# One Trainium2 core, a two-block transformer forward: the first gates' evacuation, the convolutions and their silus at other places of the hand-written order

## The chip, the cores and the metric

The kernel runs on one core of one Trainium2 chip. TensorE (PE) multiplies into PSUM banks; VectorE (DVE), ScalarE (ACT) and GpSimd (POOL) work beside it, SyncE (SP) issues DMAs. Each engine takes its own instructions in program order and waits on semaphores that other engines raise. The metric is device time in microseconds, lower is better. Before the change: 1570.03 us, median of three runs (1566.84 to 1570.04).

## The reference

One token block of 512 x 1024 goes through two layers. The first: a hybrid mixer, a cross-attention to 256 memory tokens, a squared-relu MLP. The second: a gated convolution beside a sliding-window attention, and a convolutional gated MLP. The change is in the mixer, whose core is

```python
proj = h @ w_in                       # gu, gv, q, k, v, gate, b_logit, a_logit
y_a = chunk_spatial_gating(gu, gv, ...)
qkv = silu(causal_dwconv(concat(q, k, v), dn_conv))      # 4 taps
q, k = l2norm(q), l2norm(k)                              # per head of 128
o = gated_delta_rule(q, k, v, g, beta)                   # 4 heads, triangular solves
o = rmsnorm(o, dn_onorm) * silu(gate)
out = concat(y_a, o) @ w_out
```

## The kernel before, in words

Activations lie transposed, 128 channels by 512 tokens in a tile. A projection of one output tile is 8 steps over the inner dimension, each three matmuls of 128x512 (L1308 to L1310), since weights and activations are split into a high and a low part (fp32r): 24 matmuls for a projection, 12 for a half. Projection j writes PSUM bank j mod 4 (banks 0 to 3) and may start only when the result of projection j-4 has left that bank (`evacuated`). Banks 4 to 7 are side banks; the small steps take them in turn (`side_turns`), and a step waits until the holder before it has been read.

Weights pass four slots. SP loads a slot when it is free; a `split` copies the high part on ACT (L1604) and then subtracts on DVE (L1884). SP's next load waits for both.

One list, `SCHEDULE`, sets the order of everything: `schedule()` writes (kind, number) steps, and each engine's program walks the list and issues its own share of every step. So where a step stands in the list sets its place in the queues of PE, ACT, DVE and POOL at once.

The steps that matter here (numbers 0 to 3 are heads; qkv tile n is q for 0 to 3, k for 4 to 7, v for 8 to 11):

- `conv n`: DVE takes the projection out of its bank (L1869), ACT scales it (L1667), DVE adds three taps (L1876).
- `shape n`: ACT applies silu (L1671), behind the taps. `sums n` (q and k): PE turns the tile (L1381), which needs `shape n`; ACT squares it with a sum (L1679).
- `gate n`: DVE takes the gate out of its bank (L1869 into `gate`), ACT applies silu (L1707). Gates 0 and 1 are projections 3 and 4, so gate 0 holds bank 3, the bank of projection 7 (k of head 1 is 6, v of head 1 is 7).
- The delta heads: `decay h` (PE L1235, ACT exp L1713, DVE L2030 and L2034, ACT exp L1716), `strict h` (PE L1411, nine DVE instructions, L2042 to L2059), `turn h` (PE L1420, DVE L2062), then `level_y` and `level_x` for levels 1 to 6 (PE L1437 and L1465/L1470; ACT copies y, L1721; DVE subtracts, L2089/L2090), `solve h`. The level_x of a level needs ACT's copy of y; the level_y of the next needs DVE's subtraction.
- `root` and `row` of the second block's first norm: PE turns the sum of squares that POOL has added up (L1229), DVE and POOL form the root, PE spreads it (L1235). They stand between the projections k2 and q2.

A projection is issued in halves, and the generators for projections and heads are advanced in turn, one half projection to one head step. On ACT, functions of different table sets (silu, exp, gelu) need an ACT_TABLE_LOAD between them.

Of the kernel before, what the change touches and what calls it, by code (L numbers as in the profile page):

```python
# [17 lines left out]
KT = D // P  # L18
# [4 lines left out]
H = 4  # L23
# [4 lines left out]
F2T = 2816 // P  # L28
# [10 lines left out]
SLOTS = 4  # L39
LEAD = SLOTS - 1  # L40
# [18 lines left out]

ON_DVE = (A_INPUT, *HALF_OF)  # L60

LAST_TILES = [slice(0, 3), slice(3, 6), slice(6, KT)]

GATES_BEHIND = {0: (0, 1), 1: (2,)}
# [64 lines left out]
N_LOADS = N_PROJ - KEPT  # L131
FIRST_EXTRA = N_LOADS - (KEPT - SLOTS)
PROJ = {(name, n, k0): j for j, (name, n, k0, k1) in enumerate(WEIGHTS)}
# [58 lines left out]
def schedule():  # L192

    out, done, split = [], set(), [0]

    def add(kind, n=0):
        out.append((kind, n))

    def split_ahead(j):
        while split[0] < min(j + LEAD + 1, N_LOADS) and (split[0] < SLOTS or split[0] - SLOTS in done or (  # L200
                split[0] >= FIRST_EXTRA and PROJ["gate2", F2T - 1, 0] in done)):
            add("split", split[0])
            split[0] += 1

    def project(name, n, k0=0, ka=None, kb=None):
        j = PROJ[name, n, k0]
        ka, kb = WEIGHTS[j][2] if ka is None else ka, WEIGHTS[j][3] if kb is None else kb
        if j < FRONT:
            done.add(j)
            return  # L210
        split_ahead(j)
        add("mm", (j, ka, kb))
        if kb == WEIGHTS[j][3]:
            done.add(j)
# [2 lines left out]
        add("split", j)  # L217
        split[0] = j + 1

    aside, convolved, normed_heads = [], [], []  # L220

    def halves_and_aside(name, n):
        project(name, n, kb=KT // 2)
        while convolved:
            add("shape", convolved.pop(0))
        if aside:
            aside.pop(0)()
        yield
        project(name, n, ka=KT // 2)
        if aside:  # L230
            aside.pop(0)()

    def conv_qkv(n):
        if PROJ["qkv", n, 0] not in done:
            yield from halves_and_aside("qkv", n)
        yield
        add("conv", n)
        convolved.append(n)

    def scaled(h):  # L240
        add("norms", h)
        normed_heads.append(h)

    def projections():
        for h in range(1, H):
            yield from conv_qkv(h)
            yield from conv_qkv(H + h)
            aside.extend([lambda h=h: add("sums", h), lambda h=h: add("sums", H + h), lambda h=h: scaled(h)])
            yield from conv_qkv(2 * H + h)
            for n in GATES_BEHIND.get(h, ()):  # L250
                yield from halves_and_aside("gate", n)
                add("gate", n)
                yield
        norm = memory_norm()
        for n in range(H):
            for name in GATING[n]:
                yield from halves_and_aside(name, n)
                if name == "gu":
                    if n == 0:
                        add("mix_bias")  # L260
                    add("spatial_u", n)
                else:
                    add("spatial_v", n)
                    aside.extend([lambda n=n: add("statistics", n), lambda n=n: add("normalise", n), lambda n=n: add("mix", n)])
                yield
                if n or name == "gv":
                    next(norm, None)
        last = halves_and_aside("gate", H - 1)
        next(last)
        for t in range(KT):  # L270
            add("stage", (A_MEMORY, t))
        yield
        for _ in last:
            pass
        add("gate", H - 1)
        yield
        while aside:
            aside.pop(0)()
            yield
# [57 lines left out]
    def first_memory_keys():  # L337
        yield from memory_keys(range(EARLY_KEYS))
# [35 lines left out]
    project("gate", 1, ka=KT // 2)  # L374

    ahead = PROJ["qkv", 1, 0]
    add("mm", (ahead, 0, 1))
    add("sums", H)
    add("decays")
    add("mm", (ahead, 1, KT - 2))  # L380
    first = delta_head(0)
    next(first)
    add("mm", (ahead, KT - 2, KT))
    done.add(ahead)
    add("sums", 0)
    scaled(0)
    add("shape", 2 * H)
    filler = itertools.chain(projections(), first_memory_keys())
    aside.extend([lambda: add("gate", 0), lambda: add("gate", 1)])
    in_flight, waiting = [first], list(range(1, H))  # L390
    while waiting or in_flight:
        next(filler, None)
# [37 lines left out]
    for n in range(2, KT):  # L430
        project("xa_wq", n)
        add("query", n)
        h = n // XT - 1
# [26 lines left out]
    for p, (k0, k1) in enumerate(FFN_PARTS):  # L460
# [7 lines left out]
        for n in range(KT):  # L468
            project("ffn_w2", n, k0)
            add("residual", (("ffn_w2", k0), n))  # L470
            if k1 == FT:
                normed(A_SECOND, n)
                add("square2", n)
    project("k2", 0)
    add("root", A_SECOND)
    project("q2", 0, kb=KT // 2)
    add("root", A_TWICE)
    project("q2", 0, ka=KT // 2)
    add("row", A_SECOND)

    for n in (QT, 0):
# [101 lines left out]
    add("row", A_LAST)  # L583
    for n in range(len(LAST_TILES)):
        add("final", (A_LAST, n))
# [225 lines left out]
def build_program(nc, x_in, mem_in, front_in, logits_in, weights_in, ws_in, columns_in, rows_in, sinks_in, matrices_in,  # L811
                  positions_in, out):
    with ExitStack() as base:
# [6 lines left out]
        def signal(name, kind, per=1):  # L820
            return Signal(semaphore(name), kind, per if callable(per) else lambda n: per)
# [45 lines left out]
        gate = sbuf("gate", [P, H, S], stack=delta)  # L867
# [28 lines left out]
        q2 = sbuf("q2", [P, QT, S], stack=second)  # L896
        k2 = sbuf("k2", [P, S], stack=second)
# [104 lines left out]
            signal("statistics_pe", "statistics"), signal("statistics_dve", "statistics", 2 * NC + 1), signal("statistics_pool", "statistics"))  # L1002
        normalise_dve = signal("normalise_dve", "normalise")
        mix_pe, mix_dve = signal("mix_pe", "mix"), signal("mix_dve", "mix", 2)
        gate_dve, gate_act = signal("gate_dve", "gate"), signal("gate_act", "gate")
        decay_pe, decay_act, decay_dve = signal("decay_pe", "decay"), signal("decay_act", "decay", 2), signal("decay_dve", "decay", 2)
        strict_pe, strict_dve = signal("strict_pe", "strict"), signal("strict_dve", "strict", 9)
        turn_pe, turn_dve = signal("turn_pe", "turn"), signal("turn_dve", "turn")
# [578 lines left out]
        def scalar_program(act):  # L1587
# [7 lines left out]
            for kind, n in SCHEDULE:  # L1595
                if kind == "split":
# [3 lines left out]
                    elif n >= SLOTS:  # L1600
                        name, i, k0, k1 = WEIGHTS[n - SLOTS]
# [100 lines left out]
                elif kind == "spatial_v":  # L1702
                    q.wait_ge(*spatial_v_dve.at(n))
                    act.activation(temp("v", n), temp("v", n), ACT.Gelu_apprx_tanh).then_inc(spatial_v_act.handle, 1)
                elif kind == "gate":
                    q.wait_ge(*gate_dve.at(n))
                    act.activation(gate[:, n, :], gate[:, n, :], ACT.Silu).then_inc(gate_act.handle, 1)  # L1707
                elif kind == "decay":
# [8 lines left out]
                elif kind == "level_y":  # L1717
                    h, level = n
# [126 lines left out]

            for n in range(0, len(LAST_TILES), 2):
                q.wait_ge(*final_dve.at((A_LAST, n)))
                act.dma_start(out_tiles[:, LAST_TILES[n], HALF_OF[A_LAST]], xs[:, LAST_TILES[n], HALF_OF[A_LAST]]).then_inc(out_landed.handle, 16)

        def vector_program(dve):  # L1850
# [28 lines left out]
            for kind, n in SCHEDULE:  # L1879
# [434 lines left out]
                elif kind == "final" and n[0] == A_LAST:  # L2314
                    tiles = LAST_TILES[n[1]]
                    part = xs[:, tiles, HALF_OF[A_LAST]]
# [71 lines left out]
        def sync_program(sp):  # L2388
# [131 lines left out]
```

## Time and profile before

| what | value |
|---|---|
| runs | 1566.84, 1570.03, 1570.04 us |
| the profiled execution: its time, its span | 1569.95 us, 1568.2 us |
| PE busy | 1543.0 us, 98% of the span |
| DVE, ACT, POOL busy | 878.0, 601.8, 104.9 us |
| granted TensorE clock, mean | 0.993 of full |
| HBM | 143.29 MB read, 93 GB/s over the span |

A busy PE share of 98% leaves only some 25 us of idle time to be had or lost, so the table of who waited for whom on PE, and the stretches of lower clock, say where a change of order can act. Most of them lie in the first 210 us.

### The profile page before, as it was taken

The numbers are of one execution on the slowest core, as the hardware profiler recorded it, in microseconds if no ns is written. First come the engines' busy times: TensorE is split into PE (matmuls) and PEld (weight loads), VectorE is DVE, ScalarE is ACT, GpSimd is POOL, SyncE is SP. The second block draws the span as 40 slices with busy tenths as digits, with TensorE's granted clock in tenths as the row PEclk, the third lists the DMA queues.
The fourth block names the chain that finished last, engine by engine and source line by source line (L and its number), as shares of the span: only waits on it lengthen the run. The fifth ranks groups of instructions, "written<-read, shape, count | busy, mean of one in ns | idle before, by whom it ended". The sixth has DMA issues, their size and how long they took to land.

```text
span 1568.2 us, 20461 instructions
## 1 busy us (share of the span) xinstructions
PE 1543.0 (98%) x8150; PEld 1275.4 (81%) x8150; DVE 878.0 (56%) x1331; ACT 601.8 (38%) x975; POOL 104.9 (7%) x91
## 2 busy tenths in 40 slices
PE   9898999999999999999999999999999999999998
PEld 7687789888788888888888877877888888888887
DVE  7676666654364344445565777644555663564465
ACT  6534333533344132322446344432334331332233
POOL 0000111220030000000040010100002000000000
PEclk9998999999999999999999999999999999999999
DMA  7211113531132322232332223221332233222221
GB/s 265 68 55 41 55 55 109 188 107 59 36 113 90 107 90 99 94 104 78 108 108 81 81 81 108 74 94 62 107 113 89 95 107 102 87 99 102 95 71 64
DMA packets 44941, 146.70 MB, mean 94 GB/s; under 512 B 5040, under 2 KB 8368, under 8 KB 44720
## 3 DMA queue, kind: packets, MB, share of 16 engines
q1 hardware_dynamic: 42448, 141.80, 26.8%
q10 hardware_dynamic: 2400, 3.61, 0.7%
q8 instruction: 65, 1.06, 0.3%
q14 instruction: 28, 0.23, 0.1%
HBM read 143.29 MB, written 2.10 MB: 93 GB/s over the span
## 4 chain that ended last, share of the span: by engine, by line
PE 87%; DVE 6%; ACT 4%; issue 3%; DMA 1%; POOL 0%; SPq 0%; DVEq 0%; POOLq 0%; ACTq 0%
PE bank L1308 26%; PE bank L1310 26%; PE bank L1309 26%; DVE w_lo L1884 1%; PE bank L1526 1%; PE bank L1543 1%; ACT w_hi L1604 1%; DVE temp L1876 1%; PE bank L1437 1%; PE bank L1465 1%; DVE temp L1869 1%; PE bank L1470 1%; PE bank L1273 0%; PE bank L1275 0%; PE bank L1274 0%
## 5 line engine op out<-in xcount | busy, mean ns | idle before, releaser
L1308 PE MATMUL bank<-a_hi,w_hi 128*128 128x512 f32 (+1 forms) x1275 | 499.3, 392 | 6.0 <-DVE gate L1869 6.0
L1310 PE MATMUL bank<-a_hi,w_lo 128*128 128x512 f32 (+1 forms) x1275 | 491.3, 385 | 0.0
L1309 PE MATMUL bank<-a_lo,w_hi 128*128 128x512 f32 (+1 forms) x1275 | 491.2, 385 | 0.0
L1884 DVE TENSOR_TENSOR w_lo<-w_raw,w_hi 128x1024 fp32r<-128x1024 f32 (+2 forms) x259 | 330.3, 1276 | 171.4 <-ACT w_hi L1604 171.0
L1604 ACT ACTIVATE w_hi<-w_raw 128x1024 fp32r<-128x1024 f32 (+2 forms) x259 | 267.0, 1034 | 198.3 <-PE bank L1310 195.0
L1308 PEld LDWEIGHTS bank<-a_hi,w_hi 128*128 128x128 f32 x1275 | 240.6, 189 | 57.5 <-issue 9.9
L1310 PEld LDWEIGHTS bank<-a_hi,w_lo 128*128 128x128 f32 x1275 | 240.4, 189 | 48.5
L1309 PEld LDWEIGHTS bank<-a_lo,w_hi 128*128 128x128 f32 x1275 | 240.9, 189 | 45.6
L1308 PE MATMUL bank<-b_hi,w_hi 128*128 128x512 f32 (+1 forms) x720 | 276.7, 384 | 0.4 <-ACT b_hi L1744 0.4
L1309 PE MATMUL bank<-b_lo,w_hi 128*128 128x512 f32 (+1 forms) x720 | 275.1, 382 | 0.0
L1310 PE MATMUL bank<-b_hi,w_lo 128*128 128x512 f32 (+1 forms) x720 | 275.1, 382 | 0.0
L1308 PEld LDWEIGHTS bank<-b_hi,w_hi 128*128 128x128 f32 x720 | 135.3, 188 | 28.4 <-issue 1.7
L1310 PEld LDWEIGHTS bank<-b_hi,w_lo 128*128 128x128 f32 x720 | 135.3, 188 | 26.3
L1309 PEld LDWEIGHTS bank<-b_lo,w_hi 128*128 128x128 f32 x720 | 135.4, 188 | 26.1 <-issue 0.2
L2156 DVE TENSOR_TENSOR xs<-xs,bank 128x512 f32<-128x512 f32 (+1 forms) x88 | 55.9, 637 | 135.0 <-PE bank L1310 130.9
L1869 DVE TENSOR_TENSOR temp<-bank,rstd 128x512 f32<-128x512 f32 x101 | 69.4, 687 | 62.5 <-PE bank L1310 58.0
L1876 DVE SCALAR_TENSOR_TENSOR temp<-temp,columns 128x512 f32<-128x512 f32 x96 | 72.3, 753 | 35.0 <-ACT temp L1841 17.2
L2344 POOL TENSOR_TENSOR square_sum<-square_sum,square 128x512 f32<-128x512 f32 x28 | 39.5, 1410 | 612.5 <-ACT square L1639 612.5
L2134 DVE TENSOR_TENSOR b_lo<-temp,b_hi 128x512 fp32r<-128x512 f32 x62 | 42.9, 692 | 59.3 <-ACT b_hi L1744 59.0
L1744 ACT ACTIVATE b_hi<-temp 128x512 fp32r<-128x512 f32 x62 | 39.2, 633 | 82.5 <-DVE temp L2313 56.7
L1784 ACT ACTIVATE temp<-temp 128x512 f32<-128x512 f32 x32 | 20.2, 632 | 89.4 <-DVE temp L2209 89.4
L2335 POOL TENSOR_TENSOR narrow<-narrow,columns 128x4 f32<-128x4 f32 (+1 forms) x13 | 18.5, 1423 | 422.0 <-DVE narrow L1927 382.9
(317 smaller groups left out, 1196.2 us busy)
## 6 DMA issues: line engine op xcount, KB each, us to landing
w_raw<-weights_in SPq DMA_DIRECT2D x247, 512.0 KB, 3.2
w_raw<-weights_in SPq DMA_DIRECT2D x8, 384.0 KB, 2.9
x_first<-x_in SPq DMA_DIRECT2D x8, 256.0 KB, 5.8
xs<-x_in ACTq DMA_DIRECT2D x8, 256.0 KB, 5.0
w_raw<-weights_in SPq DMA_DIRECT2D x8, 256.0 KB, 2.7
mem_x<-mem_in SPq DMA_DIRECT2D x1, 1024.0 KB, 7.7
out<-xs SPq DMA_DIRECT2D x8, 128.0 KB, 1.8
w_raw<-front_in SPq DMA_DIRECT2D x5, 192.0 KB, 6.1
```

The costliest lines, as they stand in the source:

```text
L1308: pe.matmul(to, weights_hi[:, at], hi, start=k == k0, stop=False)
L1309: pe.matmul(to, weights_hi[:, at], lo, start=False, stop=False)
L1310: t = pe.matmul(to, weights_lo[:, at], hi, start=False, stop=k == k1 - 1)
L1604: act.activation(split_weights(n)[0][:, 0:size], raw[:, n % SLOTS, 0:size], ACT.Copy).then_inc(split_act.handle, 1)
L1744: act.activation(b_hi[:, b_slot(g, i), :], x, ACT.Copy).then_inc(b_act.handle, 1)
L1784: act.activation(temp("relu", n), temp("relu", n), ACT.Square).then_inc(relu_act.handle, 1)
L1869: return dve.tensor_tensor(to, full(name, n, k0)[0:to.shape[0], 0:width], scale[0:to.shape[0], 0:width], ALU.mult)
L1876: dve.scalar_tensor_tensor(acc, buf[:, at:at + S], weight(i), acc, ALU.mult, ALU.add).then_inc(done.handle, 1)
L1884: dve.tensor_tensor(lo[:, 0:size], raw[:, n % SLOTS, 0:size], hi[:, 0:size].bitcast(F32), ALU.subtract).then_inc(split_dve.handle, 1)
L2134: dve.tensor_tensor(lo, x, hi.bitcast(F32), ALU.subtract).then_inc(b_dve.handle, 1)
L2156: dve.tensor_tensor(xs[:, t, tokens], xs[:, t, tokens], full(name, t, k0)[:, 0:tokens.stop - tokens.start], ALU.add).then_inc(residual_dve ...
L2344: pool.tensor_tensor(total, total, square("square", n)[:, 0:total.shape[1]], ALU.add).then_inc(square_pool.handle, 1)
```

## The change

It reorders steps; the work of each stays the same.

1. Gates 0 and 1 leave their banks right behind `decays`, ahead of `decay 0`; their silus (a step `silu` of its own now) stand behind `shape 8`. `norms 0` and `strict 0` come ahead of `sums 0`, and the first part of projection 5 is two inner steps long, not one.
2. The DVE work `conv n` comes half a projection later: between the halves of the next projection, behind the head's step. `shape n` comes another half later, ahead of the next `split`.
3. One call of `project` splits at most one weight tile.
4. `sums` of k, `statistics`/`mix` of group 0 are moved by a half.
5. The root of the second block's norm stands in the middle of k2, not behind it; the second root behind k2.
6. The last output tiles leave in four pieces (1, 2, 3 and 2 tiles), not three (3, 3, 2).

```diff
-LAST_TILES = [slice(0, 3), slice(3, 6), slice(6, KT)]
+LAST_TILES = [slice(0, 1), slice(1, 3), slice(3, 6), slice(6, KT)]
...
-    def split_ahead(j):
-        while split[0] < min(j + LEAD + 1, N_LOADS) and (split[0] < SLOTS or split[0] - SLOTS in done or (
-                split[0] >= FIRST_EXTRA and PROJ["gate2", F2T - 1, 0] in done)):
-            add("split", split[0])
-            split[0] += 1
+    def split_ahead(j, most=SLOTS):
+        for _ in range(most):
+            if split[0] < min(j + LEAD + 1, N_LOADS) and (split[0] < SLOTS or split[0] - SLOTS in done or (
+                    split[0] >= FIRST_EXTRA and PROJ["gate2", F2T - 1, 0] in done)):
+                add("split", split[0])
+                split[0] += 1
...
     def halves_and_aside(name, n):
-        project(name, n, kb=KT // 2)
         while convolved:
             add("shape", convolved.pop(0))
+        project(name, n, kb=KT // 2, most=1)
         if aside:
             aside.pop(0)()
         yield
-        project(name, n, ka=KT // 2)
+        while projected:
+            add("conv", projected[0])
+            convolved.append(projected.pop(0))
+        project(name, n, ka=KT // 2, most=1)
...
     def conv_qkv(n):
         if PROJ["qkv", n, 0] not in done:
             yield from halves_and_aside("qkv", n)
+        projected.append(n)
         yield
-        add("conv", n)
-        convolved.append(n)
...
-            aside.extend([lambda h=h: add("sums", h), lambda h=h: add("sums", H + h), lambda h=h: scaled(h)])
+            aside.append(lambda h=h: add("sums", h))
+            aside.extend([lambda: None, lambda h=h: add("sums", H + h), lambda h=h: scaled(h)])
...
-    add("mm", (ahead, 0, 1))
+    add("mm", (ahead, 0, 2))
     add("sums", H)
     add("decays")
-    add("mm", (ahead, 1, KT - 2))
+    for n in GATES_BEHIND[0]:
+        add("gate", n)
+    add("mm", (ahead, 2, 5))
     first = delta_head(0)
     next(first)
-    add("mm", (ahead, KT - 2, KT))
+    add("mm", (ahead, 5, KT))
     done.add(ahead)
+    scaled(0)
+    next(first)
     add("sums", 0)
-    scaled(0)
     add("shape", 2 * H)
+    for n in GATES_BEHIND[0]:
+        add("silu", n)
     filler = itertools.chain(projections(), first_memory_keys())
-    aside.extend([lambda: add("gate", 0), lambda: add("gate", 1)])
...
-    project("k2", 0)
+    project("k2", 0, kb=KT // 2)
     add("root", A_SECOND)
-    project("q2", 0, kb=KT // 2)
+    project("k2", 0, ka=KT // 2)
     add("root", A_TWICE)
-    project("q2", 0, ka=KT // 2)
+    project("q2", 0)
     add("row", A_SECOND)
```

What this makes of the queues, at three places. First DVE, about 42 to 60 us. `small` and `narrow` are per-head scalars, L1869 into `temp` is a projection taken out of its bank, into `gate` a gate. Before:

```order
L1957 TENSOR_TENSOR small<-small 128x16
L2030 TENSOR_TENSOR decays_t0<-bank6,small 128x512
...
L2059 TENSOR_TENSOR qkv<-qkv,temp2 128x512
L1869 TENSOR_TENSOR temp3<-bank1,rstd 128x512
L1967 MEMSET temp3 128x3
L1876 SCALAR_TENSOR_TENSOR temp4<-temp3,columns,temp4 128x512 x3
L1884 TENSOR_TENSOR w_lo<-w_raw,w_hi 128x1024 x2
L1869 TENSOR_TENSOR gate<-bank3,rstd 128x512
L1869 TENSOR_TENSOR gate<-bank0,rstd 128x512
```

And the same place now:

```order
L1970 TENSOR_TENSOR small<-small 128x16
L1882 TENSOR_TENSOR gate<-bank3,rstd 128x512
L1882 TENSOR_TENSOR gate<-bank0,rstd 128x512
L2043 TENSOR_TENSOR decays_t0<-bank6,small 128x512
...
L2072 TENSOR_TENSOR qkv<-qkv,temp2 128x512
L1987 TENSOR_SCALAR narrow<-narrow 128x4
L1897 TENSOR_TENSOR w_lo<-w_raw,w_hi 128x1024
L2075 COPY inv_b0<-bank6 128x256
L1882 TENSOR_TENSOR temp3<-bank1,rstd 128x512
```

The two gates stand ahead of the decay now; one split and the turn's copy stand ahead of the first convolution.

Second ACT, around the decay of head 2. L1721 (now L1734) copies a level's y, the L1713 pair (L1726) and L1716 (L1729) are the two exps of the decay, L1671 (L1684) a silu, L1604 (L1617) a split, L1679 (L1692) the squares of `sums`. Before:

```order
L1604 ACTIVATE w_hi<-w_raw 128x1024
L1671 ACTIVATE qkv<-temp4 128x512
L1679 ACTIVATE square1,narrow<-bank4 128x128 x4
L1721 ACTIVATE level_y1<-bank5 128x256
L1713 ACT_TABLE_LOAD
L1713 ACTIVATE temp0<-bank6 128x512
L1716 ACTIVATE decays_t0<-decays_t0 128x512
L1679 ACTIVATE square0,narrow<-bank7 128x128 x4
```

And now:

```order
L1734 ACTIVATE level_y1<-bank5 128x256
L1726 ACT_TABLE_LOAD
L1726 ACTIVATE temp3<-bank6 128x512
L1729 ACTIVATE decays_t0<-decays_t0 128x512
L1684 ACT_TABLE_LOAD
L1684 ACTIVATE qkv<-temp2 128x512
L1617 ACTIVATE w_hi<-w_raw 128x1024
L1692 ACTIVATE square1,narrow<-bank7 128x128 x4
```

The silu of tile 3 (q of head 3), the split and the squares of that tile stand behind both exps now, with a table load ahead of the silu.

Third PE at the second block's norm. Bank 0 is k2, bank 1 is q2, `square_sum` is what POOL adds up. Before:

```order
L1308 MATMUL bank0<-a_hi,w_hi 128x512
L1309 MATMUL bank0<-a_lo,w_hi 128x512
L1310 MATMUL bank0<-a_hi,w_lo 128x512
L1229 MATMUL bank4<-matrices,square_sum 128x128 x4
L1308 MATMUL bank1<-a_hi,w_hi 128x512
```

And now:

```order
L1321 MATMUL bank0<-a_hi,w_hi 128x512
L1322 MATMUL bank0<-a_lo,w_hi 128x512
L1323 MATMUL bank0<-a_hi,w_lo 128x512
L1242 MATMUL bank7<-matrices,square_sum 128x128 x4
L1321 MATMUL bank0<-a_hi,w_hi 128x512
```

The turn of the sum of squares is 12 matmuls earlier: bank 0 stands on both sides of it.

## Rows read from the trace of the kernel before

**Rows 1.** Waits of PE over the span: us in total, times, longest.
```profile
PE bank L1308 <- DVE gate L1869: 6.0, 1, 6.0
PE bank L1411 <- ACT square L1679: 2.8, 1, 2.8
PE bank L1420 <- DVE k_dec L2082: 1.7, 1, 1.7
PE bank L1470 <- DVE temp L2010: 1.4, 1, 1.4
...
PE bank L1381 <- ACT qkv L1671: 0.6, 1, 0.6
...
PE bank L1459 <- ACT level_y L1721: 0.5, 1, 0.5
PE bank L1229 <- DVE inv_t L2095: 0.5, 1, 0.5
...
PE bank L1411 <- DVE decays_t L2030: 0.4, 1, 0.4
```
**Rows 2.** Stretches: length, busy PE, PEld, DVE, ACT, POOL, granted clock, DMA share, GB/s.
```profile
55.70:62.60 6.90, 2.92 (x7) 2.37 (x8) 6.03 (x10) 3.80 (x6) 0.00 (x0) 0.51 0.46 151
...
137.60:141.10 3.50, 3.50 (x17) 3.50 (x17) 1.73 (x5) 0.00 (x0) 0.99 (x1) 0.51 0.00 0
...
151.30:158.10 6.80, 6.17 (x28) 4.99 (x29) 4.42 (x10) 1.57 (x2) 0.00 (x0) 0.50 0.22 79
```
**Rows 3.** Timeline of DVE, 48 to 60 us: start, length, instruction, idle before.
```profile
48.50 0.68 DVE L2042 TENSOR_TENSOR decays_t<-decays_t,small 128x512 f32<-128x512 f32 x1
...
52.86 0.68 DVE L1869 TENSOR_TENSOR temp<-bank,rstd 128x512 f32<-128x512 f32 x1
...
56.58 2.35 DVE L1884 TENSOR_TENSOR w_lo<-w_raw,w_hi 128x1024 fp32r<-128x1024 f32 x2
58.84 1.28 DVE L1869 TENSOR_TENSOR gate<-bank,rstd 128x512 f32<-128x512 f32 x2
```
**Rows 4.** Timeline of PE, 67.5 to 74 us.
```profile
68.38 0.68 PE L1465 MATMUL bank<-inv_tb,level_y 64*64 64x64 f32 x16
...
69.46 0.50 PE L1308 MATMUL bank<-a_hi,w_hi 128*128 128x512 f32 x1
...
72.43 0.68 PE L1437 MATMUL bank<-inv_b,level_b 64*64 64x64 f32 x16
```
**Rows 5.** Timeline of all engines, 131.8 to 137.5 us, decay of head 2.
```profile
131.85 0.40 ACT L1721 ACTIVATE level_y<-bank 128x256 f32<-128x256 f32 x1
...
132.27 1.28 ACT L1713 ACT_TABLE_LOAD   x1
...
133.56 0.60 ACT L1713 ACTIVATE temp<-bank 128x512 f32<-128x512 f32 x1
...
135.64 0.63 ACT L1716 ACTIVATE decays_t<-decays_t 128x512 f32<-128x512 f32 x1 [1.48 <-DVE decays_t L2034]
```
**Rows 6.** Timeline of ACT, 71 to 75 us.
```profile
71.81 1.04 ACT L1604 ACTIVATE w_hi<-w_raw 128x1024 fp32r<-128x1024 f32 x1
74.31 0.63 ACT L1671 ACTIVATE qkv<-temp 128x512 f32<-128x512 f32 x1 [1.45 <-DVE temp L1876]
```
**Rows 7.** Timeline, 809 to 823.5 us: k2 begins, second block's norm.
```profile
809.65 0.39 PE L1308 MATMUL bank<-a_hi,w_hi 128*128 128x512 f32 x1
...
813.45 1.40 POOL L2344 TENSOR_TENSOR square_sum<-square_sum,square 128x512 f32<-128x512 f32 x1 [3.04 <-ACT square L1639]
...
815.09 0.60 PE L1229 MATMUL bank<-matrices,square_sum 128*128 128x128 f32 x4
...
822.60 1.09 PE L1235 MATMUL bank<-matrices,narrow 128*128 128x128 f32 x8 [0.96 <-POOL narrow L2357]
```
**Rows 8.** Timeline of all engines, 1562 to 1568 us, the end.
```profile
1562.33 2.42 DVE L2319 TENSOR_TENSOR xs<-xs,bank 128x768 f32<-128x768 f32 x3 [1.30 <-PE bank L1235]
1563.31 1.86 ACTq L1848 DMA_DIRECT2D out<-xs  x2
```

More of the change, by code:

```diff
@@ L197, in add, with project @@
         out.append((kind, n))
-    def split_ahead(j):
-        while split[0] < min(j + LEAD + 1, N_LOADS) and (split[0] < SLOTS or split[0] - SLOTS in done or (
-                split[0] >= FIRST_EXTRA and PROJ["gate2", F2T - 1, 0] in done)):
-            add("split", split[0])
-            split[0] += 1
-    def project(name, n, k0=0, ka=None, kb=None):
+    def split_ahead(j, most=SLOTS):
[4 more added lines that the diff above has]
+                split[0] += 1
+    def project(name, n, k0=0, ka=None, kb=None, most=SLOTS):
         j = PROJ[name, n, k0]
@@ L210, in project @@
             return
-        split_ahead(j)
+        split_ahead(j, most)
         add("mm", (j, ka, kb))
@@ L218, in first_split @@
         split[0] = j + 1
-    aside, convolved, normed_heads = [], [], []
+    aside, projected, convolved, normed_heads = [], [], [], []
     def halves_and_aside(name, n):
-        project(name, n, kb=KT // 2)
         while convolved:
             add("shape", convolved.pop(0))
+        project(name, n, kb=KT // 2, most=1)
         if aside:
@@ L263, in projections @@
                     add("spatial_v", n)
-                    aside.extend([lambda n=n: add("statistics", n), lambda n=n: add("normalise", n), lambda n=n: add("mix", n)])
+                    aside.extend([lambda n=n: add("statistics", n), lambda n=n: add("normalise", n)])
+                    if n == 0:
+                        aside.append(lambda: None)
+                    aside.append(lambda n=n: add("mix", n))
                 yield
@@ L275, in projections @@
         add("gate", H - 1)
+        add("silu", H - 1)
         yield
@@ L376, in schedule @@
     ahead = PROJ["qkv", 1, 0]
-    add("mm", (ahead, 0, 1))
+    add("mm", (ahead, 0, 2))
     add("sums", H)
     add("decays")
-    add("mm", (ahead, 1, KT - 2))
+    for n in GATES_BEHIND[0]:
+        add("gate", n)
+    add("mm", (ahead, 2, 5))
     first = delta_head(0)
     next(first)
-    add("mm", (ahead, KT - 2, KT))
+    add("mm", (ahead, 5, KT))
     done.add(ahead)
+    scaled(0)
+    next(first)
     add("sums", 0)
-    scaled(0)
     add("shape", 2 * H)
+    for n in GATES_BEHIND[0]:
+        add("silu", n)
     filler = itertools.chain(projections(), first_memory_keys())
-    aside.extend([lambda: add("gate", 0), lambda: add("gate", 1)])
     in_flight, waiting = [first], list(range(1, H))
@@ L1004, in build_program @@
         mix_pe, mix_dve = signal("mix_pe", "mix"), signal("mix_dve", "mix", 2)
-        gate_dve, gate_act = signal("gate_dve", "gate"), signal("gate_act", "gate")
+        gate_dve, gate_act = signal("gate_dve", "gate"), signal("gate_act", "silu")
         decay_pe, decay_act, decay_dve = signal("decay_pe", "decay"), signal("decay_act", "decay", 2), signal("decay_dve", "decay", 2)
@@ L1704, in scalar_program @@
                     act.activation(temp("v", n), temp("v", n), ACT.Gelu_apprx_tanh).then_inc(spatial_v_act.handle, 1)
-                elif kind == "gate":
+                elif kind == "silu":
                     q.wait_ge(*gate_dve.at(n))
```

## The prediction, written before the changed kernel was run

> **What bounds the kernel now.** I read the page first: PE is busy 1543.0 of 1568.2 us, so work moved off PE is worth nothing and only PE's waits can change. Next the waits of PE [rows 1]: eight in the mixer, 13.9 us together with their second decimals (6.05, 2.84, 1.66, 1.37, 0.63, 0.54, 0.46, 0.36). The reader should see one large and several small ones. Then the stretches by granted clock [rows 2]: three in the mixer at half rate (1.2 GHz), each behind PE's waits. Half of what PE was busy in them is their price: 2.92/2 + 3.50/2 + 6.17/2 = 6.3 us. So 20.2 us can be got back there at most. Last the timelines, for the lengths.
>
> The 6.05 us stand at 53.6 to 59.7 us. Projection 7 needs bank 3, which gate 0 holds; DVE takes the gate out at 58.84, behind head 0's nine strict instructions, convolution 1 and two splits [rows 3].
>
> **Units for the sums.** Strict on DVE: 52.86 - 48.50 = 4.4 us. A convolution on DVE, leave to last tap: 56.58 - 52.86 = 3.8. A DVE split 1.15 (2.35 for two), a gate's leave 0.6 (1.28 for two) [rows 3]. A half projection on PE: 72.43 - 69.46 = 2.97; a level_x 69.46 - 68.38 = 1.1 [rows 4]; level_y, strict and decay on PE I take as 0.6, 1.8 and 0.45 (16 small matmuls are half a level_x; the other two are 16 and 4 matmuls of 128 columns, at their pitch of 0.11 between them). ACT from its copy of y to the end of a decay's second exp: 136.27 - 131.85 = 4.4; a table load 1.28 [rows 5]; silu 0.63, ACT split 1.04 [rows 6].
>
> **Part 1, the gates.** Their two leaves (1.3 us) fall into the time in which DVE waits for the first exp of decay 0, so they cost nothing; if that cover were gone they would delay the decay by 1.3. The 6.05 us go, with 1.5 us of half rate behind them, and 0.6 at `sums 4`, since three more matmuls (0.7) cover the wait for its silu. What is late next: DVE's split 8 now stands ahead of turn 0 and waits for ACT, which has silus 8, gate 0, gate 1 (a table load and 3 x 0.6) ahead of it. By my sum strict 0 ends on DVE at 50.2, ACT's split at 52.4, DVE's at 53.6, the turn's copy at 54.0; PE wants level_y at 53.5 and waits 0.6. Convolution 1 then ends at 57.8, its silu at 58.5, and PE waits 0.8 for it. PE is 5.7 us ahead here.
>
> **Part 2, convolution and silu behind the heads' steps.** In a plain cycle PE needs two halves, sums, a level_y and a level_x: 8.1 to 8.2 us. DVE needs 3.8 (convolution) + 0.4 + 1.15 + 0.1 + 0.7 = 6.1, but the silu is now ahead of the split on ACT, and it waits for the last tap: 0.65 + 1.05 between DVE's last tap and its split, of which DVE fills 0.4. That makes 7.5, so plain cycles pass without a wait but with 0.6 us to spare instead of 2. Where a head begins, they don't pass:
> - Head 1. DVE has convolution 9, the norms and gate 2's leave ahead; silu of gate 2 ends 3.8 us after PE has finished projection 8. Then copy, two exps (4.4), the silu of tile 9 with a table load (1.9), the split (1.05): PE waits 0.2 for the copy, 1.55 for the bank that DVE's first decay instruction frees, 1.55 for level_x's subtraction, which stands behind a split on DVE: 3.3.
> - Head 2. From the end of PE's level_y: 4.4 + 0.1, a table load 1.28, silu 0.63 = 6.5 us to the silu of tile 3, while PE wants it after a decay and a half, 3.4: a wait of 3.05. The split (1.04) and four squares (1.15) hold strict 2's second bank: 0.55. DVE's strict (4.4) then stands ahead of convolution 7 (3.8): 1.65 at `sums 7`; and mix_bias, behind convolution 11 and the norms, holds the bank of level_y(2,1): 1.7. Together 7.0.
> - Head 3. Its decay needs the bank of `statistics 0` until DVE has normalised: 0.5; `mix 0` 0.25. Strict 3 on DVE begins behind a split that waits for ACT's exps, then mix and v's leave, gelu: `statistics 1` wants it 2.6 earlier. level_y(2,5) is given the bank of `statistics 1` and waits for its normalisation: 2.2. Together 5.5.
> - The end: level_y(3,5) 0.6; and `state 0` now follows `solve 3` at once, with no projection between, and waits for ACT's copy: 0.8. Together 1.4.
>
> With 1.6 from part 1 that is 18.8 us of waits, against 13.9 now. Bounds for this sum, which no row of before shows: the heads' beginnings may cost nothing new (only the plain waits: 3) or all of it and the 2 us by which I let queues recover twice (23). I take 18.8, since its lengths are rows and the engines' orders are known. Splits limited to one for each call, and the moved sums, have their price in these figures; later loads cost nothing, as a weight is split three projections ahead of its use.
>
> **Clock.** The present waits of 6.05 and 2.84 us were each followed by half rate, and a busy 3.5 us at half rate cost 1.7 [rows 2]. Behind the waits of 3.05, 2.6 and the pair at head 1 I expect the same three times, 5.1, and take half, 2.6: while PE runs slowly the engines it waits for go on. Bounds: 0 and 6.3, what it costs now.
>
> **Part 3, the second norm.** k2 begins at 809.65, its middle is 12 x 0.227 later, at 812.4. The turn there needs POOL's last sum, which ends at 814.85 [rows 7]. PE waits 2.5. Today it has work until 815.09, and waits 0.96 later, for the root [rows 7]. The root's chain is not the earlier for it, since DVE reads the bank only at 817.1, behind a split. So k2 and q2 end at about 824.0 and the spread begins then, not at 822.60: +1.4. Bounds: 0 (if POOL's sum came 2.5 earlier) and 3.1 (half rate behind the wait).
>
> **Part 4, the last tiles.** DVE's four pieces take as long as its three, 2.4 us and one fixed part [rows 8]. The first DMA is issued some 0.5 us sooner, at 1562.8 and not 1563.31. As the other pieces still leave behind it one after the other, and the last is issued no sooner, I take -0.3, between -0.6 and +0.3.
>
> **The sum.** 18.8 + 2.6 - 20.2 + 1.4 - 0.3 = +2.3 us. The profiled execution took 1569.95 us (span 1568.2 and 1.75 around it) and is at the median of 1570.03, so the forecast is **1572.3 us**.
>
> **A rule weighed.** A table load took 1.28 us, and the exp began 0.01 us behind it [rows 5]. The Trainium skill ("ScalarE: Activation LUTs", What ACT_TABLE_LOAD costs) gives some 1.28 us for the load and 1.38 more for a drain. By the page the two switches in head 2's chain would add 2.8 us to its wait, and as much in head 1's, and the sum would be about +8; by the row it is +2.3. This trace has no such drain.
>
> **Rivals.**
> - The cover holds. The copies of y come ahead of the silus, so a level's PE step never waits for a tap; if DVE keeps up better than I reckon at head 2 and head 3, the new waits are 9 and half rate costs 1.7: 9 + 1.7 - 20.2 + 1.1 = -8.4, some 1562; with part of it, 1564. For it: from 62.6 to 134 us PE has waited 0.4 in all, with DVE two thirds busy. Against it: the order on ACT puts a silu and a split behind both exps.
> - The clock falls. Place: head 2, `sums 3` to level_y(2,1), four waits within 30 us. If half rate follows three of them in full (today one is followed by two such stretches, 6.8 us), and head 1's and the norm's too, it costs 9 rather than 2.6: 1579. It decides once PE's waits of 1.5 to 3 us are enough for it. For it: the 1.66 was followed by 6.8 us. Against: 1.37 at 174 was not [rows 1, 2].
> - The gates' early leave does not do what it says: projection 7's bank is free, but PE waits as long for the first silus, so the start gains 2 rather than 8 us while later stretches lose little: 1570.
>
> **Chances.** Forecast 0.52, with a range of its own from 1568 to 1577; cover 0.24; clock 0.12; no gain at the gates 0.12. A difference under 0.2% (3.1 us) can't be told from none. Slower than 1573.2: 0.22 of the forecast's 0.52, all of the clock's 0.12, 0.01; faster than 1566.9: 0.22 of the cover's 0.24, 0.01. So 0.23 faster, 0.42 the same, 0.35 slower. The range of 1564 to 1578 leaves out a part of the first and second rival.
>
> **What would show it.** Right: no wait of PE near 53 to 60 us, gate leaves on DVE near 43; a wait near 125 us at L1381 (`sums 3`) of 2.5 to 3.5 with a table load and silu before it; one of about 2.5 at L1229 near 812 and none at the spread; PE's idle time in the mixer 16 to 21 us. Wrong: that idle time below 10, or strict 2's bank as the longest wait still, or PE less than 4 us ahead by level_x(0,1).

## The result, and the profile after

The changed kernel took 1577.42 us (median of 5 runs, 1576.55 to 1579.22), the kernel before 1569.06 us (5 runs, 1566.84 to 1570.04): a ratio of 1.0055 with a 95% interval of 1.0044 to 1.0067. That is 8.4 us slower, where +2.3 (1572.3) was forecast; it lies within the range of 1564 to 1578, and 0.4 us above the forecast's own range of 1568 to 1577. The profiled execution took 1576.55 us (span 1574.8), 6.6 more than that of before. Of all executions in this document the ratios leave out one, of `gates_turn`, which took 2204.46 us at a mean granted clock of 0.65, where its five others took 1561.74 to 1564.17 us at 0.997 to 0.999.

The waits of PE in the mixer (38 to 260 us: us in total, times, longest), which answer to [rows 1]. Below, level_y(h,l) is the `level_y` of head h at level l.

```profile
PE bank L1394 <- ACT qkv L1684: 6.0, 3, 3.4
PE bank L1401 <- ACT temp L1717: 2.4, 1, 2.4
PE bank L1450 <- DVE inv_b L2102: 2.1, 1, 2.1
PE bank L1450 <- DVE inv_tb L2103: 1.5, 1, 1.5
PE bank L1424 <- DVE decays_t L2043: 1.4, 1, 1.4
PE bank L1450 <- DVE temp L2023: 0.9, 1, 0.9
PE bank L1517 <- ACT qkv L1738: 0.7, 1, 0.7
PE bank L1450 <- DVE inv_b L2075: 0.6, 1, 0.6
...
```

One wait of 6 us has become many of 0.6 to 3.4; with two of 0.3 more they come to 16.2 us, against 13.9. The longest is the one at `sums 3` (L1394). ACT's timeline ahead of it (start, length, instruction, idle before) shows the chain of decay 2, and the silu of tile 3 behind it:

```profile
122.11 0.38 ACT L1734 ACTIVATE level_y<-bank 128x256 f32<-128x256 f32 x1 [1.45 <-PE bank L1450]
122.72 1.28 ACT L1726 ACT_TABLE_LOAD   x1 [0.23 <-PE bank L1248]
124.02 0.60 ACT L1726 ACTIVATE temp<-bank 128x512 f32<-128x512 f32 x1
126.10 0.63 ACT L1729 ACTIVATE decays_t<-decays_t 128x512 f32<-128x512 f32 x1 [1.48 <-DVE decays_t L2047]
126.75 1.28 ACT L1684 ACT_TABLE_LOAD   x1
128.04 0.63 ACT L1684 ACTIVATE qkv<-temp 128x512 f32<-128x512 f32 x1
128.58 1.04 ACT L1617 ACTIVATE w_hi<-w_raw 128x1024 fp32r<-128x1024 f32 x1
```

The stretches at half clock (1.2 GHz; columns as in [rows 2]); three are in the mixer, behind the waits of 3.4, 1.9 and 2.4 us, and one is new, behind the second norm's:

```profile
129.50:132.90 3.40, 3.40 (x40) 3.28 (x40) 2.66 (x5) 1.18 (x9) 0.00 (x0) 0.50 0.27 75
143.10:146.50 3.40, 3.40 (x49) 3.09 (x46) 3.10 (x7) 1.06 (x9) 1.01 (x1) 0.50 0.33 86
187.50:190.90 3.40, 3.40 (x40) 2.99 (x35) 2.65 (x9) 0.58 (x1) 0.68 (x2) 0.50 0.12 33
819.00:822.40 3.40, 3.40 (x12) 2.72 (x10) 2.71 (x3) 0.00 (x0) 1.43 (x2) 0.50 0.10 23
```

The second norm on PE, against [rows 7]: the wait stands at k2's middle, and the matmuls behind it take 0.63 us each, not 0.39.

```profile
818.68 0.88 PE L1242 MATMUL bank<-matrices,square_sum 128*128 128x128 f32 x4 [2.34 <-POOL square_sum L2357]
819.21 0.77 PE L1321 MATMUL bank<-a_hi,w_hi 128*128 128x512 f32 x1
819.78 0.63 PE L1322 MATMUL bank<-a_lo,w_hi 128*128 128x512 f32 x1
...
829.42 0.82 PE L1248 MATMUL bank<-matrices,narrow 128*128 128x128 f32 x6
```

The end, against [rows 8]:

```profile
1568.62 0.43 PE L1248 MATMUL bank<-matrices,narrow 128*128 128x128 f32 x2 [1.02 <-POOL narrow L2348]
1569.09 2.48 DVE L2332 TENSOR_TENSOR xs<-xs,bank 128x256 f32<-128x256 f32 x4 [1.30 <-PE bank L1248]
1569.54 1.87 ACTq L1861 DMA_DIRECT2D out<-xs  x2
```

Where the 6.6 us of the two profiled executions lie, by the start of the same matmul in both:

| up to | before | after | added in the stretch |
|---|---|---|---|
| the recurrence's first matmul (`state 0`) | 250.94 | 254.65 | +3.7 |
| 2560 matmuls later (w_out to the FFN's end) | 807.84 | 811.64 | +0.1 |
| the second norm's spread | 822.60 | 829.42 | +3.0 |
| the last row's spread | 1561.86 | 1568.62 | -0.1 |
| the end of the span | 1568.2 | 1574.8 | -0.2 |

### The profile page after: what moved, and what is told of

It reads as the page before. It is cut to its first block, busy times and chain, and to the rows that moved or that the text cites. A ratio compares the mean times of both kernels' runs of the same rounds, so it can differ in the third digit from the quotient of the medians.

```text
span 1574.8 us, 20474 instructions
## 1 busy us (share of the span) xinstructions
PE 1546.7 (98%) x8150; PEld 1276.2 (81%) x8150; DVE 877.9 (56%) x1332; ACT 604.2 (38%) x977; POOL 104.6 (7%) x91
## 4 chain that ended last, share of the span: by engine, by line
PE 87%; DVE 5%; issue 4%; ACT 3%; POOL 1%; POOLq 0%; DVEq 0%; ACTq 0%
PE bank L1321 26%; PE bank L1323 25%; PE bank L1322 25%; PE bank L1539 1%; PE bank L1556 1%; DVE temp L1889 1%; POOL square_sum L2357 1%; ACT w_hi L1617 1%; PE bank L1478 1%; PE bank L1450 1%; DVE temp L1882 1%; PE bank L1286 0%; PE bank L1288 0%; PE bank L1287 0%; DVE w_lo L1897 0%
## 5 line engine op out<-in xcount | busy, mean ns | idle before, releaser
L1617 ACT ACTIVATE w_hi<-w_raw 128x1024 fp32r<-128x1024 f32 (+2 forms) x259 | 267.2, 1034 | 202.5 <-PE bank L1323 196.9
L1797 ACT ACTIVATE temp<-temp 128x512 f32<-128x512 f32 x32 | 20.2, 632 | 89.4 <-DVE temp L2222 89.4
```

Source lines behind the costliest of these rows:

```text
L1617: act.activation(split_weights(n)[0][:, 0:size], raw[:, n % SLOTS, 0:size], ACT.Copy).then_inc(split_act.handle, 1)
L1797: act.activation(temp("relu", n), temp("relu", n), ACT.Square).then_inc(relu_act.handle, 1)
```

## The experiments

"The mixer" is here the time on PE from the first `sums` to `state 0`. Its rows come from a view that takes one stretch of each kernel (columns as in [rows 2]). Its idle time is the length less PE's busy time; what half clock costs is half of PE's busy time in the half-clock stretches, as in the prediction. (The wait of 0.63 at before's first `sums` lies just ahead: with it 13.3 is the 13.9 of the forecast.)

| kernel | median us | ratio to before, 95% | mixer | idle | half clock costs |
|---|---|---|---|---|---|
| before (profiled) | 1569.06 | | 211.9 | 13.3 | 6.3 |
| second norm's order alone | 1570.49 | 1.0013 [1.0004, 1.0021] | 208.8 | 13.3 | 2.7 |
| gates' part alone | 1565.85 | 0.9982 [0.9973, 0.9991] | 208.3 | 10.8 | 4.6 |
| late convolutions alone | 1580.81 | 1.0074 [1.0061, 1.0086] | 219.1 | 20.0 | 5.5 |
| changed | 1577.42 | 1.0055 [1.0044, 1.0067] | 215.0 | 16.2 | 5.1 |
| changed, norm as before | 1576.25 | 1.0044 [1.0030, 1.0057] | 217.6 | 17.5 | 6.4 |
| changed, zeros at the norm's wait | 1575.18 | 1.0041 [1.0028, 1.0053] | 216.2 | 17.6 | 5.1 |
| gates' part, convolution 1 behind turn 0 | 1563.82 | 0.9964 [0.9951, 0.9977] | 205.3 | 10.0 | 1.7 |

Rows of four of them, in the order before, second norm's order alone (the same mixer), changed, changed with the norm as before (again one mixer):

```profile
39.02:250.94 211.92, 198.64 (x1903) 166.06 (x1904) 142.40 (x310) 88.41 (x190) 14.64 (x16) 0.96 0.18 58
```

```profile
38.81:247.57 208.76, 195.43 (x1903) 163.06 (x1904) 142.37 (x310) 88.57 (x190) 14.67 (x16) 0.98 0.18 59
```

```profile
39.63:254.65 215.02, 198.79 (x1901) 164.27 (x1900) 143.36 (x311) 90.29 (x192) 14.16 (x16) 0.98 0.18 60
```

```profile
39.65:257.20 217.55, 200.07 (x1902) 164.94 (x1901) 143.40 (x311) 90.37 (x192) 14.18 (x16) 0.97 0.18 59
```

The same instructions in the same order differ by 3.2 and 2.5 us from one execution to the next. Of the 3.2 all is PE's busy time at another granted clock; of the 2.5 half is (1.3), and the other half is waits (1.2). One of them makes the difference: level_y(2,5) waits 0.88 us in the changed kernel's trace, where a stretch at half clock lies between it and `statistics 1`, and 2.43 in the two other traces of the same mixer, where none does. In `after_norm_back`:

```profile
PE bank L1450 <- DVE temp L2023: 2.4, 1, 2.4
```

So one profiled execution gives the mixer's half clock only as one sample, and with it the waits that follow a stretch at half clock; the others agree to 0.05 us.

**1. The second norm, put back.** `after_norm_back`:
```diff
-    project("k2", 0, kb=KT // 2)
+    project("k2", 0)
     add("root", A_SECOND)
-    project("k2", 0, ka=KT // 2)
+    project("q2", 0, kb=KT // 2)
     add("root", A_TWICE)
-    project("q2", 0)
+    project("q2", 0, ka=KT // 2)
```


> The changed kernel with k2, q2 and the two roots of the second norm in the order of the kernel before; all else as changed. Theory A (a new wait costs itself and half of what PE is busy at 1.2 GHz behind it): 2.34 us of wait against 0.96, and 1.7 of half rate, go: 3.1 us less than the changed kernel, 1574.3, and 1.0035 of the kernel before. The rival (waits alone, the clock would have fallen anyway): 1.4 us less, 1576.0. If PE only moves its waiting elsewhere: no difference.

1576.25. From the 2560th matmul to the spread the trace shows 14.77 us (814.19 to 828.96), as before's 14.76, against 17.78 in the changed kernel: 3.0 less, as theory A has it. The median fell by 1.2 only, which by itself would fit the rival (1576.0); executions of one mixer differ by more than that, so the trace decides here.

**2. The second norm's order alone.** `before_norm`: the reverse edit, on the kernel before.

> The kernel before with the second norm's order alone changed (root at k2's middle, second root at k2's end). Theory A: +1.4 of wait and +1.7 of half rate, 1572.1 against 1569.1, with a wait of 2.3 for POOL's sum and 3.4 us of half clock behind it. The rival: +1.4, 1570.5, no stretch at half clock. Cover: +0, the wait at the spread for the wait at the root.

1570.49, 1.9 above the 1568.57 of the runs beside it; the interval (0.6 to 3.3 us) holds both sizes. The trace decides: 804.47 to 822.25 is 17.78 us again, +3.0, with PE's wait of 2.36 and this stretch behind it.

```profile
812.40:815.80 3.40, 3.40 (x10) 2.66 (x9) 2.23 (x4) 0.00 (x0) 1.32 (x2) 0.50 0.27 76
```

Both traces with that order show the half clock there. That every execution pays it is not shown: both medians (1.2 in experiment 1, 1.9 here) are nearer to the wait alone, 1.4.

**3. Zeros in the norm's wait.** `after_norm_busy`:
```diff
                 elif kind == "root":
                     q.wait_ge(*first_matrices_landed.at())
+                    if n == A_SECOND:
+                        wait_side("sum", n)
+                        for _ in range(10):
+                            pe.matmul(side("sum", n)[:, 0:P], warm[:, 0:P], warm[:, P:2 * P], start=True, stop=True)
                     q.wait_ge(*summed(n))
```


> The changed kernel with 10 matmuls of zeros (128x128, some 2.1 us together) ahead of the wait for POOL's sum at k2's middle, into the bank that the root then overwrites: PE waits as long but isn't idle. Theory A: no half clock behind it, 1.7 us less than the changed kernel, 1575.7, though the wait itself is there. The rival (half rate there is no answer to PE's idleness): 1577.4, with the stretch at half clock still there.

1575.18. PE's timeline:

```profile
817.18 2.40 PE L1347 MATMUL bank<-warm 128*128 128x128 f32 x20
819.69 0.66 PE L1242 MATMUL bank<-matrices,square_sum 128*128 128x128 f32 x4
820.11 0.48 PE L1321 MATMUL bank<-a_hi,w_hi 128*128 128x512 f32 x1
820.42 0.40 PE L1322 MATMUL bank<-a_lo,w_hi 128*128 128x512 f32 x1
```

The turn comes as late (7.05 us behind the 2560th matmul, 7.04 in the changed kernel), but the matmuls behind it run at full rate: 812.64 to 828.83 is 16.19 us, 1.6 less than 17.78. So, as far as one trace with zeros against two without can show it, the half clock there answers PE's idleness, and nearly its whole price of 1.7 reaches the spread. The median is 2.2 less than the changed kernel's; the intervals of the two ratios overlap.

**4. The same in the mixer.** `after_mixer_busy` (norm as before):
```diff
                 elif kind == "sums":
                     wait_side("sums", n)
+                    for _ in range({3: 15, 7: 8}.get(n, 0)):
+                        pe.matmul(side("sums", n)[:, 0:P], warm[:, 0:P], warm[:, P:2 * P], start=True, stop=True)
```
and ten ahead of `statistics 1`.

> The changed kernel with the second norm as before (1576.3) and matmuls of zeros (128x128) ahead of three waits of the mixer: 15 at sums 3 (about 3.1 us of 3.4), 8 at sums 7, 10 at statistics 1. PE waits as long, but isn't idle. Theory A (each half clock in the mixer is the answer to PE's idleness just before): the three stretches (5.1 to 6.4 us in the two traces of this mixer) shrink to one, behind the wait of 2.4 at level_y(2,5) which stays; 1572 to 1573. The rival (half rate comes there whatever PE does): 1576, with the same stretches.

1575.92 (1.0046 [1.0034, 1.0058]), with no gain over 1576.25. The places behind the three waits are at full clock (first three rows). Half clock comes behind level_y(2,5) (fourth row), and a second time, against the expectation, for 3.4 us behind level_y(3,5), at 238.45:

```profile
128.00:131.40 3.40, 3.34 (x51) 2.90 (x50) 0.87 (x1) 3.39 (x11) 0.00 (x0) 1.00 0.00 0
142.50:146.00 3.50, 3.50 (x58) 3.06 (x58) 3.10 (x7) 1.30 (x9) 1.01 (x1) 1.00 0.20 69
187.00:190.40 3.40, 3.40 (x45) 2.92 (x40) 2.71 (x9) 0.52 (x1) 0.64 (x1) 1.00 0.13 36
194.10:197.50 3.40, 3.40 (x20) 2.70 (x16) 0.83 (x1) 2.53 (x6) 1.27 (x2) 0.50 0.02 5
```

Theory A holds for the clock at these places and fails for the time. Two waits behind them:

```profile
PE bank L1455 <- DVE temp L2028: 2.4, 1, 2.4
PE bank L1455 <- DVE mix_bias L1979: 1.6, 1, 1.6
```

PE, now faster behind `sums 7`, waits 1.57 us at level_y(2,1), where the changed kernel waited 0.35; and 2.42 at level_y(2,5), where it waited 0.88. The kernel to compare with is `after_norm_back`: against its trace half clock costs 3.0 us less (3.4, not 6.4), but 1.57 at level_y(2,1) and 0.33 at strict 2 are new, level_y(2,5) waits as long as there (2.43), and the mixer is 1.0 us shorter (216.5, not 217.6). So a stretch at half clock behind `sums 7` takes at least 1.2 us out of the next wait, and one behind `statistics 1` takes 1.5, each at a price of 1.7: in the mixer most of what half rate takes is time that PE would have waited for DVE anyway.

**5. The gates' part alone.** `before_gates`: point 1 of the change on the kernel before (the preamble of the diff, the step `silu`).

> The kernel before with the first gates' part alone: gates 0 and 1 leave their banks ahead of decay 0 on DVE, their silus follow the shape of tile 8, norms and strict 0 ahead of the first sums; convolutions, shapes, splits, second norm and last tiles as before. Theory A (this part is the gain, and the shift of convolutions and silus eats it): the 6.05 us of wait and 1.5 of half rate go, waits of 0.6 and 0.8 come, and the later stretches stay as they are: 6 us less than the kernel before, 1563. The rival (PE's lead is lost again whatever the order, since DVE and ACT limit the heads): the waits come back at heads 1 and 2, under 2 us less, 1567 to 1569.

1565.85: 2.7 us less, under half of what was expected. The three longest waits of its mixer:

```profile
PE bank L1443 <- DVE inv_b L2068: 3.6, 1, 3.6
PE bank L1443 <- DVE temp L2016: 2.1, 1, 2.1
PE bank L1465 <- DVE k_dec L2088: 1.1, 1, 1.1
```

The 6.05 are gone, but level_y(0,1) waits 3.62 for the turn's copy, which DVE does behind convolution 1 and two splits. The waits behind it come to 7.0 us, against 7.2 before. So neither theory as written: what is missing is lost at once, at turn 0, and not at heads 1 and 2.

**6. Convolution 1 behind turn 0.** `gates_turn`, on the last:
```diff
     def conv_qkv(n):
         if PROJ["qkv", n, 0] not in done:
             yield from halves_and_aside("qkv", n)
+        if n == 1:
+            projected.append(n)
         yield
-        add("conv", n)
-        convolved.append(n)
+        if n > 1:
+            if n == H + 1:
+                add("shape", convolved.pop(0))
+            add("conv", n)
+            convolved.append(n)
```
with `projected` emptied between the halves, as in the change, and one split ahead of projection 6.

> The kernel before with the first gates' part, and convolution 1 behind turn 0 with one split ahead of it (as in the changed kernel, for this tile alone); all other convolutions and silus, the second norm and the last tiles as before. Theory A (the shift pays at turn 0, where PE waited 3.6 us for the copy behind convolution 1 and two splits, and costs at heads 1 to 3): that wait falls to 0.6, the half clock behind it goes; 3 to 5 us less than with the gates alone (1565.9), 1561 to 1563. The rival (what PE gains there it waits at head 1, since DVE's work up to strict 1 is the limit): 1565 to 1566.

1563.82, 0.9964 of before: faster than both kernels, and 2.0 us less than the gates alone, where 3 to 5 (theory A) or under 1 (the rival) was expected. The 3.62 became 0.58; 1.5 us come back at once (0.51 and 0.95 at 64 to 65 us).

**7. The late convolutions alone.** `before_late`: points 2 to 4 of the change, gates where they were.

> The kernel before with the second part alone (convolutions half a projection later, silus ahead of the splits, one split for each call, the moved sums and mix 0); gates 0 and 1 leave where they did, norm and last tiles as before. Gate 0 then leaves ahead of convolution 1 and behind one split, so the wait of 6.05 shrinks to about 1.5. Theory A (the waits at heads 1 to 3, 9 to 10 us with what follows, are this part's own, whoever is ahead): 1568.6 - 4.5 + 9 = 1573, with waits of 3.4 at sums 3 and over 2 at level_y(3,5). The rival (they are PE's lead of 6 us, spent again): waits there of under 5 us in all, 1565 to 1567.

1580.81, 11.9 us slower, the slowest of all. Its mixer's waits:

```profile
PE bank L1388 <- ACT qkv L1678: 4.2, 2, 3.6
PE bank L1427 <- DVE mix_bias L1968: 3.9, 1, 3.9
PE bank L1444 <- DVE inv_b L2096: 2.1, 1, 2.1
PE bank L1477 <- DVE temp L2017: 2.0, 1, 2.0
...
PE bank L1477 <- DVE k_dec L2089: 1.6, 1, 1.6
PE bank L1395 <- ACT temp L1711: 1.4, 1, 1.4
PE bank L1315 <- DVE gate L1876: 1.2, 1, 1.2
```

The gate's wait is 1.2, as expected, and the others are this part's own, since PE has hardly a lead to spend here (`sums 1` at 62.59 us, before at 63.84): theory A, and larger. The largest stand elsewhere than in the changed kernel (3.6 at `sums 1`, 3.9 at mix_bias's bank); of the two places that theory A named, `sums 3` doesn't wait and level_y(3,5) does, 2.08. With the gates' part in place the rest of the change costs 10.4 us and not 11.9 (`after_norm_back`'s 1576.25 against 1565.85).

**8 and 9. ACT's order.** `after_silu_first` puts `while convolved: add("shape", ...)` ahead of `add("decay", h)`; `after_split_first` puts `project` ahead of it in `halves_and_aside`. Both have the norm as before.

> The changed kernel with the second norm as before (1576.3) and the silus of tiles 9 and 3 ahead of the exps of decays 1 and 2 on ACT, not behind them. Theory A (the longest wait, 3.4 at sums 3, is that silu standing behind two exps and two table loads): that wait falls under 0.5, the half clock behind it goes (2.9), the exps and with them strict 1 and 2 come 0.5 to 1 later: 1571 to 1573. The rival (DVE's load sets the heads' beginning, whatever stands first on ACT): the wait comes back at strict 2 or level_y(1,5) in full, 1576.

1573.47 (mixer 214.5, idle 17.5). The wait at `sums 3` is gone, and PE waits 2.89 behind it, for strict 2's bank:

```profile
PE bank L1426 <- ACT square L1694: 2.9, 1, 2.9
```

The rival in the main: this is the wait of 2.84 that the kernel before had at that place [rows 1]. ACT's exps come late for PE here too; the silu only got in front of them. The 2.8 us less in the median are no more than executions of one mixer differ by; ratio 1.0035 [1.0023, 1.0047], an interval that overlaps that of 1576.25.

> The changed kernel with the second norm as before (1576.3) and ACT's split ahead of the silu again in each projection; convolutions stay half a projection late. Theory A (the silu is what PE waits for at heads 1 and 2): it stands 1.0 later, the wait at sums 3 grows to 4.4 and waits of up to 1 come at the other sums; 1577 to 1580. The rival (the silu ahead of the split makes DVE's splits late, and with them the subtractions, so that it is what made the waits of 1.4, 1.5, 2.4 and 2.1 at strict and level_y): 3 to 4 less, 1572.

1575.08 (1.0035 [1.0023, 1.0047]). `sums 3` waits 4.34, 0.95 more, as theory A has it, and `sums 1` and 7 as in the changed kernel; but the 1.48 at level_y(0,4) is gone, since DVE's split ahead of that subtraction no longer waits for ACT's table load and silu (it begins at 80.79, in the changed kernel at 82.50). The two nearly cancel. Both theories missed the sum.

**10 and 11. Around the fastest version.** `turn_tiles` adds the four last tiles, `turn_normalise` also puts each `normalise` right behind its `statistics`.

> The fastest version so far (first gates' part, convolution 1 behind turn 0; 1563.8) with four last tiles. Theory A: 0.3 less from the last row's spread to the end (6.2 us, not 6.5), 1563.5, too little to show in a ratio. The rival: 0, since the DMAs leave one after another.

> As turn_tiles, with each normalise right behind its statistics, half a projection earlier, on DVE ahead of the decay's products. Theory A (level_y(2,3) waits 2.07 for the bank that statistics 0 holds until DVE has normalised behind decay 3's exp): that wait and the half clock behind it go, 1561. The rival (DVE then waits for POOL's variances, which holds up level_x(2,2)'s subtractions and decay 3): the wait moves to strict 3, 1563 to 1565.

1563.87 and 1564.04 (ratios 0.9970 [0.9959, 0.9981] and 0.9973 [0.9964, 0.9982]), no different from 1563.82. The tiles can't be told from nothing in time; from the last spread to the span's end the traces show 6.15 to 6.41 us with four pieces (eight traces) and 6.3 to 6.6 with three (five). With the early `normalise` the wait of 2.07 at level_y(2,3) shrinks to 0.95, but three later level_y wait 0.41, 0.39 and 1.50 us: the rival. `turn_tiles` had no half clock in the mixer (203.7 us) and `gates_turn` one stretch (205.3), with the same waits to 0.05 us.

## Why the prediction came out as it did

**Sign and mechanism right, the size too small: +8.4 for +2.3.** The step that failed is the sum's treatment of the clock, at both ends: 6.3 us of half rate were put down as what can be got back in the mixer, of which another execution paid only 2.7, and the half rate behind the second norm's wait was put at nothing and takes 1.7. PE's longer work at full clock was in no term.

**Part 1** held: waits of 0.60 at level_y(0,1) and 0.76 at `sums 1` (forecast 0.6, 0.8). PE's lead there, by `sums 1` (59.06 against 63.84, with a level_y of 0.6 more done), is 5.4 us for 5.7. `sums 1` before and now:

```profile
63.84 0.60 PE L1381 MATMUL bank<-matrices,qkv 128*128 128x128 f32 x4
59.06 0.41 PE L1394 MATMUL bank<-matrices,qkv 128*128 128x128 f32 x2 [0.76 <-ACT qkv L1684]
```

**Part 2** held at its large waits, with one miss. Head 1: 1.43 + 1.48 = 2.9 (forecast 3.3). Head 2: 3.40, 0, 1.86, 0.35 = 5.6 (7.0). Head 3: 2.37 + 0.88 = 3.2 (5.5). End: 0.34 + 2.06 + 0.69 = 3.1 (1.4). The two that look far too small, 0.35 for 1.7 at level_y(2,1) and 0.88 for 2.2 at level_y(2,5), follow stretches at half clock; without these they are 1.57 and 2.42 (experiment 4). So the forecast priced them nearly rightly for a PE at full rate; with 1.57 and 2.42 in place of the two the waits would come to 19.0 for 18.8, a nearness in which misses of both signs cancel. The miss is the 2.06 at level_y(3,5), forecast 0.6: eight memory tiles now stand ahead of level_x(3,4)'s subtraction on DVE, and I had not counted them.

```profile
231.11 1.36 DVE L2023 TENSOR_SCALAR temp<-bank,ln_mean 128x128 f32<-128x128 f32 x4
232.39 3.25 DVE L1913 SCALAR_TENSOR_TENSOR a_lo<-mem_x,columns,a_hi 128x256 fp32r<-128x256 f32 x8
235.55 0.41 DVE L2102 TENSOR_TENSOR inv_b<-inv_b,bank 128x256 f32<-128x256 f32 x1
```

**The clock in the mixer.** Forecast 18.8 of waits and 2.6 of clock, 21.4; measured 16.2 and 5.1, 21.3. Half rate did follow three waits in full, and took 2.8 us out of two later ones (experiment 4), so "take half" was right as a net price. Waits and clock of the mixer thus changed by the +1.2 forecast, but that is this pair of traces, and luck: over the three traces of the changed mixer they come to 21.3, 23.8 and 22.7, over the two of before's to 20.2 and 16.3, a difference of 4.4 in the mean. For the 6.3 us of half rate that were to be got back were one execution's; another of the same mixer paid 2.7, and there neither the wait of 2.85 at strict 2 nor the 1.66 was followed by half rate. A second thing was in no term. Up to `state 0` the changed kernel lost 2.5 us more that are neither waits nor half clock. Of these 0.6 are there by 38 us, ahead of every step that was moved, so they are not the change's. PE changes between kinds of matmul 250 times in the mixer and not 235, which by an estimate from the traces' mean distances accounts for 0.7; the remaining 1.2 I can't place. The three traces of the changed mixer (215.0, 217.6, 216.2) lie 5.9 above the mean of the two of before's (211.9, 208.8), not 3.1. With the norm's 3.0 and the tail's -0.2 that makes 8.7, near the medians' 8.4; with so few traces the nearness is no proof of each term.

**Part 3, the second norm: the mis-sized term.** The wait came as forecast, 2.34 for 2.5, but +3.0 and not +1.4: a busy 3.4 us at half rate follow, which I had as a bound (3.1) and left out of the value, though the wait of 2.84 in [rows 1] was followed by it. Here, unlike in the mixer, nothing gives it back: PE finds its operands ready from then on. Experiments 2 and 3 show both halves of the price.

**Part 4**: -0.2 for -0.3, with the first DMA 0.92 us behind the last spread and not 1.45.

**Rivals.** The cover didn't hold: the mixer's waits are 16.2 us and not 9, and the late convolutions alone cost 11.9 us. The gates do what they say: the 6.05 is gone and PE is 5.4 us ahead; that this part alone gained only 2.7 is the wait at turn 0 (experiment 5). The clock rival (1579) came nearest in time, and in the changed kernel's trace was right at the norm and at three of the mixer's waits; the pair at head 1 (1.43 and 1.48) was not followed by half rate, and its price of 9 was 6.8.

**The rule weighed.** In the chain above each load takes 1.28 us, and exp and silu begin 0.02 and 0.01 behind it. The drain of 1.38 us that the Trainium skill ("ScalarE: Activation LUTs", What ACT_TABLE_LOAD costs) adds is not there; that the sum by the page, +8, is near the measured +8.4 is chance, since the wait it would have lengthened measured 3.40 for 3.05.

**The expectations missed too.** I took the gates' part for 6 us and it was 2.7 (the turn's copy stood behind convolution 1 in the order, and I had not read that far), convolution 1 behind turn 0 for 3 to 5 and it was 2.0, and the late convolutions for 4.5 slower and they were 11.9.

## What to carry to other kernels

Price a change's waits by reading what stands ahead of the awaited instruction on each engine, every staged tile included: that gave the five largest waits but one to within 0.4 us. Then ask of each long wait what PE meets behind it: where it soon waits for others again, half rate costs little net; where everything is ready, add half of the stretch in full. Don't book the half clock of a single trace as a gain: here it was 6.3 us in one execution and 2.7 in another. And price a part on its own, not only the whole: here one part gained 2.7 us, one lost 11.9, and a single step of the second (convolution 1) was what the first needed. The parts' prices don't add up: with the norm's 3.0 and the tail's -0.2 they would make 12.0, and the whole is 8.4.

## What the runs showed of the hardware that was not expected

The same order of instructions drew half clock for 17.1 us of one execution's mixer and 6.8 us of another's (211.9 and 208.8 us long); behind the waits of 2.84 at strict 2 and 1.66 at turn 2 one trace shows half rate and the other doesn't. In the three traces of the changed mixer the waits of 3.40 at `sums 3` and 1.9 at `sums 7` were followed by it each time, that of 2.37 at `statistics 1` once, that of 2.43 at level_y(2,5) both times that it came, and that of 2.1 at level_y(3,5) never; but in `after_silu_first` and `after_mixer_busy` level_y(3,5) (2.08) was followed by it, and `sums 7` (1.85) in the former was not. So the length of a wait alone doesn't settle it. Matmuls of zeros were enough to keep the clock up: at the norm 2.4 us of them in place of idle time left 1.00 behind, where the same wait idle left 0.50 in two traces.

DVE's split takes 1.23 us (at 229.97 in the changed kernel) and 2.23 where POOL adds squares at the same time (at 813.06; it ends 1.08 us behind POOL's instruction, which ends at 814.21). All seven splits of that trace that begin within 0.2 us of such an add took 2.19 to 2.24 us. No run takes POOL's work away, so that it is the cause is not tested.
